# One chunk of a 31-tap convolution: from TensorE (products with diagonals) to ScalarE (products) and GpSimd (sums)

## The reference, cut to what matters

```python
zc = z[..., o4:]
glu = zc[..., :D_C] * jax.nn.sigmoid(zc[..., D_C:])
conv_c, new_c = causal_dwconv(glu, prev_c, w_conv_c)      # 31 taps, one weight per tap and channel
y_c = jax.nn.silu(layernorm(conv_c + b_conv_c, g_ln_c, b_ln_c))
```

## Time and profile before

| | |
|---|---|
| median of 3 runs | 1135.69 us (1135.05 to 1145.3) |
| profiled execution, own time | 1139.49 us |
| its span on the core | 1137.9 us |
| mean granted TensorE clock | 0.983 |
| TensorE busy | 1079.7 us, 95% of the span |
| VectorE busy | 934.3 us, 82% |
| ScalarE busy | 720.0 us, 63% |
| GpSimd busy | 97.1 us, 9% |

### The profile page before, as it was taken

How to read it: one execution, slowest core, us unless ns; L and a number is a source line. 1 busy time by engine, 2 the same in 40 slices (tenths; PEclk the granted TensorE clock), 3 DMA queues, 4 the chain that set the end, 5 groups by cost and what they waited for, 6 DMA issues and landing times.

```text
span 1137.9 us, 17514 instructions
## 1 busy us (share of the span) xinstructions
PE 1079.7 (95%) x6405; PEld 954.4 (84%) x6405; DVE 934.3 (82%) x1277; ACT 720.0 (63%) x891; POOL 97.1 (9%) x120
## 2 busy tenths in 40 slices
PE   6996999999998998799999999999999999999985
PEld 5995999999998897688888888888888888888775
DVE  6998866656668699756989989899898999999765
ACT  5434544434444532646888888888888788888562
POOL 5420000000000350100001010000100001003000
PEclk9998999999999999799999999999999999999998
DMA  8522445554452333145999999999999999999910
GB/s 331 192 90 77 148 149 205 207 186 185 158 213 101 131 141 118 48 149 186 387 366 389 360 374 396 342 410 361 379 386 346 410 359 385 377 369 398 338 67 39
DMA packets 23913, 291.56 MB, mean 256 GB/s; under 512 B 3128, under 2 KB 3160, under 8 KB 6960
## 3 DMA queue, kind: packets, MB, share of 16 engines
q1 hardware_dynamic: 20464, 279.24, 64.0%
q0 software_dynamic: 3392, 11.54, 2.9%
HBM read 283.98 MB, written 6.79 MB: 256 GB/s over the span
## 4 chain that ended last, share of the span: by engine, by line
PE 74%; DVE 16%; issue 3%; DMA 3%; ACT 2%; POOL 1%; DVEq 0%; POOLq 0%; ACTq 0%; SPq 0%
PE bank L635 14%; PE bank L639 14%; PE bank L638 14%; PE bank L680 9%; PE bank L683 9%; PE bank L684 9%; DVE wlo L1318 4%; DVE cv L1392 4%; DMA sq<-y_rows,row_id 2%; PE bank L698 1%; DVE rstd L1330 1%; PE bank L579 1%; DMA y_rows<-work 1%; PE bank L752 1%; PE bank L563 1%
## 5 line engine op out<-in xcount | busy, mean ns | idle before, releaser
L1229 DVE TENSOR_TENSOR wlo<-ring,whi 128x1024 fp32r<-128x1024 f32 x384 | 460.1, 1221 | 52.5 <-ACT whi L844 45.6
L844 ACT ACTIVATE whi<-ring 128x1024 fp32r<-128x1024 f32 x384 | 404.6, 1059 | 88.4 <-PE bank L635 76.7
L635 PE MATMUL bank<-whi,gh_hi 128*128 128x512 f32 x512 | 204.5, 399 | 0.2 <-DVE wlo L1229 0.2
L639 PE MATMUL bank<-whi,gh_lo 128*128 128x512 f32 x512 | 200.2, 391 | 0.0
L638 PE MATMUL bank<-wlo,gh_hi 128*128 128x512 f32 x512 | 199.5, 390 | 0.0
L925 ACT ACTIVATE whi<-ring 128x1024 fp32r<-128x1024 f32 x137 | 143.4, 1051 | 77.9 <-PE bank L680 75.3
L680 PE MATMUL bank<-hid_hi,whi 128*128 128x264 f32 x608 | 180.9, 297 | 9.1 <-ACT pp L936 4.8
L684 PE MATMUL bank<-hid_hi,wlo 128*128 128x264 f32 x608 | 175.2, 288 | 0.0
L683 PE MATMUL bank<-hid_lo,whi 128*128 128x264 f32 x608 | 175.1, 288 | 0.0
L1318 DVE TENSOR_TENSOR wlo<-ring,whi 128x1024 fp32r<-128x1024 f32 x137 | 166.1, 1223 | 0.4
L680 PE MATMUL bank<-gh_hi,whi 128*128 128x264 f32 x480 | 138.2, 288 | 2.8 <-DVE gh_lo L1605 1.4
(11 more groups left out here) (251 smaller groups left out, 1368.5 us busy)
## 6 DMA issues: line engine op xcount, KB each, us to landing
ring<-wstream SPq DMA_DIRECT2D x131, 2048.0 KB, 8.6
y_rows<-work POOLq DMA_DIRECT2D x7, 512.0 KB, 8.1
h<-x_in SPq DMA_DIRECT2D x1, 1056.0 KB, 5.0
y_out<-work POOLq DMA_DIRECT2D x2, 528.0 KB, 3.0
xn_rows<-work SPq DMA_DIRECT2D x2, 512.5 KB
par<-par_in SPq DMA_DIRECT2D x2, 494.5 KB, 7.0
c_sample<-xc POOLq DMA_DIRECT2D x2, 372.0 KB, 3.8
stc<-state_in SPq DMA_DIRECT2D x2, 360.0 KB, 9.2
```

Of the source, the lines that this page charges most:

```text
L635: mm = pe.matmul(out[:, :], xh, whi[:, pos, cols_], start=(k == 0), stop=False)
L639: mm = pe.matmul(out[:, :], xl, whi[:, pos, cols_], start=False, stop=(k == last))
L844: nc.scalar.activation(whi[:, q % SPLITS, :], quarter_at(q), ACT.Copy).then_inc(S["hi"], 1)
L1229: v.tensor_tensor(wlo[:, q % SPLITS, :], quarter_at(q), whi[:, q % SPLITS, :].bitcast(F32), ALU.subtract).then_inc(S["lo"], 1)
```

## The change

Chunk 0 of the convolution no longer goes through TensorE. ScalarE makes, for each tap, the product of the shifted view of `cpad` and the tap's weight: the first, with the bias, goes into `cv` itself, the other 30 into six buffers of 128x256 in `sq` (chunks 2 to 7). GpSimd adds each of the 30 to `cv`. The products come three at a time (`TAPS_ACT`) behind each of the four gelus, after the high half that precedes the square, after the layer norm's gain and behind each later high half, until 31 are made. ScalarE waits before it writes a buffer again until GpSimd has added it, and GpSimd waits for its own previous sum, since all go into the same tile. TensorE waits for the last sum ahead of the mean, in place of ScalarE's `conv_0`. The diagonals, their matmuls, and ScalarE's copy out of bank 6 go away.

```diff
-DIAGS = 12
-TAPS_PE = -(-TAPS_C // (N_ZAB - 1))
+TAPS_ACT = -(-TAPS_C // (N_ZAB - 1))
...
-        diag = sq_row[:, 2 * T:2 * T + DIAGS * P].rearrange("p (i q) -> p i q", q=P)
+        products = [sq[:, i, 0:SEQ] for i in range(2, KD)]
...
                 pool.wait_ge(S["ms"], 1)
-                for k in range(TAPS_C):
-                    if l or k >= DIAGS:
-                        pool.wait_ge(diag_used, l * TAPS_C + max(k - DIAGS + 1, 0))
-                    pool.tensor_scalar(diag[:, k % DIAGS, :], ident[:, :], col(l, "w_conv_c", k), None,
-                                       ALU.mult).then_inc(diag_ready, 1)
+                for k in range(1, TAPS_C):
+                    pool.wait_ge(tap_product, l * TAPS_C + k + 1)
+                    if k > 1:
+                        pool.wait_ge(tap_added, l * (TAPS_C - 1) + k - 1)
+                    pool.tensor_tensor(cv[:, 0, 0:SEQ], cv[:, 0, 0:SEQ], products[(k - 1) % len(products)],
+                                       ALU.add).then_inc(tap_added, 1)
...
-                tap = iter(range(TAPS_C))
-
-                def some_taps():
-
-                    for _ in range(TAPS_PE):
-                        k = next(tap, None)
-                        if k is None:
-                            return
-                        if k == 0:
-
-                            pe.wait_ge(S["glu"], 1)
-                        pe.wait_ge(diag_ready, l * TAPS_C + k + 1)
-                        pe.matmul(bank[6][:, 0:SEQ], diag[:, k % DIAGS, :], cpad[:, 0, k:k + SEQ], start=(k == 0),
-                                  stop=(k == TAPS_C - 1)).then_inc(diag_used, 1)
-
-                project(B["zab"], 2 * CB, *mix, between=some_taps)
+                project(B["zab"], 2 * CB, *mix)
...
-                pe.wait_ge(conv_0, l + 1)
+                pe.wait_ge(tap_added, (l + 1) * (TAPS_C - 1))
                 average(bank[4], D_C, average_c, S["mean"])
...
+                next_tap = iter(range(TAPS_C))
+
+                def tap_products():
+
+                    for _ in range(TAPS_ACT):
+                        k = next(next_tap, None)
+                        if k is None:
+                            return
+                        src, w = cpad[:, 0, k:k + SEQ], col(l, "w_conv_c", k)
+                        if k == 0:
+                            nc.scalar.activation(cv[:, 0, 0:SEQ], src, ACT.Identity, bias=col(l, "b_conv_c"),
+                                                 scale=w).then_inc(tap_product, 1)
+                        else:
+                            if k > len(products):
+                                act.wait_ge(tap_added, l * (TAPS_C - 1) + k - len(products))
+                            nc.scalar.activation(products[(k - 1) % len(products)], src, ACT.Copy, scale=w).then_inc(
+                                tap_product, 1)
+
+                for c in range(2 * CB):
                     high_upto(dense_quarters(B["zab"] + c))
                     act.wait_ge(acc_evac, B["zab"] + c + 1)
                     nc.scalar.activation(zb[:, c, :], ycat[:, c, :], ACT.Gelu_apprx_tanh).then_inc(S["gelu"], 1)
+                    tap_products()
                 high_upto(dense_quarters(B["zab"] + 2 * CB + 1))
+                tap_products()
                 act.wait_ge(S["centred"], 1)
...
+                tap_products()
                 for c in range(2 * CB + 2, N_ZAB):
                     high_upto(dense_quarters(B["zab"] + c))
-
-                act.wait_ge(diag_used, (l + 1) * TAPS_C)
-                nc.scalar.activation(cv[:, 0, 0:SEQ], bank[6][:, 0:SEQ], ACT.Identity,
-                                     bias=col(l, "b_conv_c")).then_inc(conv_0, 1)
+                    tap_products()
```

More of the change, by code:

```diff
@@ L204, in build @@
         spread = rstd2[:, :]
-        diag = sq_row[:, 2 * T:2 * T + DIAGS * P].rearrange("p (i q) -> p i q", q=P)
-        assert 2 * T + DIAGS * P <= KD * T
+        products = [sq[:, i, 0:SEQ] for i in range(2, KD)]
         sg = sig[:, :, :].rearrange("p b t -> p (b t)")[:, 0:512]
@@ L274, in build @@
         late_step = sem("overflow_step")
-        diag_ready = sem("diag_ready")
-        diag_used = sem("diag_used")
-        conv_0 = sem("first_chunk_convolved")
+        tap_product = sem("tap_product_ready")
+        tap_added = sem("tap_added")
         L = [{n: sem(f"{n}_{l}") for n in (
@@ L710, in _ @@
                 project(B["zc"], N_ZC, *mix, S["gh_mix"])
-                tap = iter(range(TAPS_C))
-                def some_taps():
-                    for _ in range(TAPS_PE):
-                        k = next(tap, None)
-                        if k is None:
-                            return
-                        if k == 0:
-                            pe.wait_ge(S["glu"], 1)
-                        pe.wait_ge(diag_ready, l * TAPS_C + k + 1)
-                        pe.matmul(bank[6][:, 0:SEQ], diag[:, k % DIAGS, :], cpad[:, 0, k:k + SEQ], start=(k == 0),
-                                  stop=(k == TAPS_C - 1)).then_inc(diag_used, 1)
-                project(B["zab"], 2 * CB, *mix, between=some_taps)
+                project(B["zab"], 2 * CB, *mix)
                 average(bank[5], D_B, [zb[:, c, :] for c in range(CB)], S["mean"], (S["gelu"], 1))
-                project(B["zab"] + 2 * CB, 2, *mix, between=some_taps)
+                project(B["zab"] + 2 * CB, 2, *mix)
                 pe.wait_ge(S["squared"], 1)
                 average(bank[5], D_B, [sq[:, c, :] for c in range(CB)], S["variance"])
-                project(B["zab"] + 2 * CB + 2, 3 * CA - 2, *mix, between=some_taps)
+                project(B["zab"] + 2 * CB + 2, 3 * CA - 2, *mix)
                 pe.wait_ge(S["ln_b"], CB)
@@ L963, in _ @@
                         act.wait_ge(S["glu"], 2)
-                for c in range(CB):
+                next_tap = iter(range(TAPS_C))
[14 more added lines that the diff above has]
+                for c in range(2 * CB):
                     high_upto(dense_quarters(B["zab"] + c))
```

## The result

The changed kernel takes 1165.31 us in the median (1164.14 to 1169.01, 4 runs) against 1136.61 (1135.05 to 1145.3, 4 runs): a ratio of 1.0235, 95% interval 1.0198 to 1.0273. It is slower by 2.0 to 2.7%. One execution of the kernel before took 4448.55 us in a later set of runs; the ratios leave it out.

The account below looks back on a forecast made before the run. VectorE was taken as the bound. Per layer, + 9.9 (sums) + 0.4 (late high half) - 0.4 (products with the identity) - 0.1 (TensorE's relief) = + 9.8 us; both layers + 19.6, giving 1155.3 us, range 1134 to 1174.

Parts of the forecast that it names:

- rival 2: Convolution stage: each sum holds VectorE for its whole duration, 16 to 26 us a layer, 1167 to 1187; chance 0.12.
- VectorE is the bound, TensorE's relief is worth nothing: Convolution stage: VectorE the bound by 0.3 us a chunk; TensorE's 24.8 us of taps costed at nothing.
- The sums hold VectorE, all on the chain: Convolution stage: 30 GpSimd sums a layer delay VectorE by 0.33 us each on average, 9.9 us a layer.
- the affine_select's row: GpSimd instruction over 512 elements beside a delayed VectorE tensor_scalar, from which a 0.44 us hold per sum was taken.
- The gap under a tap: Part of a hold that fits between VectorE's instructions, taken off: 0.11 us under a tap, 0.02 under a low half.
- The signs that it named: VectorE's stage groups, same counts but longer: taps 0.47 to 0.6 or 0.8 us, low halves 1.22 to some 1.5.
- The products with the identity cost 0.4 us a layer: Convolution stage: GpSimd's removed products had delayed VectorE's low halves by 0.09 us each; some 0.4 us a layer returns.
- The late high half costs 0.4 us: Seventh chunk: ScalarE's high half, behind three products, comes 1.0 us later with 0.6 to spare, adding 0.4 us.
- Sum: Whole kernel: terms give + 9.8 us a layer, + 19.6 for both, a median of 1155.3 us.
- Rival 1: Convolution stage: sums cost VectorE nothing because GpSimd gives way; 1133 to 1135 us; chance 0.24, extended to 0.19 a sum.
- Rival 3: Convolution stage: GpSimd's chain of sums becomes the bound above 1.8 us each; 1168 at 2.2; chance 0.10 with rival 4.
- Rival 4: Convolution stage: gaps halve TensorE's clock, up to 9 us more a layer, 1173; chance 0.10 together with rival 3.

Follow-up runs that it names:

- the run with other slots: Against the kernel before: ScalarE makes chunk 0's products, TensorE sums them, no GpSimd work in the stage, no taps behind the seventh chunk; 1137.27 us, ratio 0.9983.
- the half sums: Against the changed kernel: each GpSimd sum covers 128 of the 256 columns, the other half of chunk 0 left unsummed; 1146.98 us.
- the one-input run: Against the changed kernel: each GpSimd sum replaced by an in-place tensor_scalar over the same 128x256 buffer, sums left out; 1146.67 us.

## Why the prediction was right, point by point

The mechanism, the place and the direction were right. The size was not: the forecast proper was 1147 to 1163 us at 0.2 to 0.45 us a sum, and the kernel took 1165.31 at 0.45 to 0.50. The measured time lies inside the stated range of 1134 to 1174 because that range also took in part of rival 2.

- *VectorE is the bound, TensorE's relief is worth nothing.* Right, to within the few tenths of a us a layer that the run without its taps leaves open. Taking its 62 taps away changed the time by a ratio of 1.0003, and in that run, as before and after the change, no row of TensorE stands in the chain of the stage.
- *The sums hold VectorE, all on the chain.* Right in mechanism, place and sign. The step that was off is the size: 0.33 us a sum, 9.9 us a layer. It is 0.50 us in a round, and over the layer 13.4 us or 0.45 a sum. The 0.17 us that are missing in the round come from three places. The reading was taken at 0.86 ns an element from the affine_select's row (0.44 us for 512), and the held low halves show 0.55: 0.11 us. That row shows a VectorE instruction with one tensor in SBUF, the first after a wait for a DMA; no run tests whether its delay was the same hold. The gap under a tap was taken as 0.11 us and is 0.07, under a low half 0.02 and is nothing: 0.03 on average. A share of the sums was put under the evacuation, where they would be free, and none of the round's three fell there: 0.03. The signs that it named came too large as well: a low half of some 1.5 us was to be seen, and it is 1.76 in order of time.
- *The Trainium skill's figure.* The Trainium skill's "GPSIMD Engine Reference" (Performance versus the Vector engine) gives about 2.6 cycles an element for a sum, an estimate of 0.55 us here, and 13 us a layer. The runs agree with that (0.55 on a low half, 13.4 a layer), and the nearest row of the trace was the worse guide. The Trainium skill's "SBUF — State Buffer" (Who interferes with whom) is borne out where it says that only reads of GpSimd exclude a VectorE instruction with two SBUF inputs: memsets cost 0.00 us, and evacuations from PSUM kept their 0.42 us. That the other waits for the whole instruction is not: a sum, 0.74 us long in the median, held a low half for 0.55, and a one-input instruction of 0.85 us or more cost 0.17.
- *The products with the identity cost 0.4 us a layer.* They cost 0.7 (0.56 + 0.16; the run with other slots gives 0.65), and under taps they cost something in one run.
- *The late high half costs 0.4 us.* 0.67 us without sums. In the changed kernel it costs nothing, because VectorE comes later still: its low half follows its taps with no wait. ScalarE's products were hidden otherwise.
- *Sum.* + 9.8 us a layer forecast, + 12.8 measured, of which the runs account for 13.4 - 0.7 = 12.7. For the median 1155.3 us were forecast and 1165.3 measured. The sums were put 3.5 us a layer too low. By luck the products (given 0.3 too little) and the high half (0.4 too much) took 0.7 of that back.
- *Rival 1* (the sums cost nothing) and *rival 2* (the whole instruction, 16 to 26 us a layer) are out, the second by the half sums and the one-input run. In time the result is nearer to rival 2's lower edge (1167) than to the 1155 of the forecast, so the time alone could not have told them apart. Rival 1's limit of 0.19 us a sum is 11 / 60 = 0.18. *Rival 3*: a sum takes 1.0 us from start to start, at the lower end of what was expected, far from 1.8; GpSimd is not in the chain. *Rival 4*: the clock did fall, to 0.82 at the lowest, and cost nothing, since TensorE's work still fitted into the longer rounds.

## What to carry to other kernels

Work put on an idle GpSimd isn't free when VectorE is the bound and reads two operands from SBUF: count the elements that GpSimd's sums read, both inputs, at about 1.1 ns each, as VectorE's time (a one-input instruction cost about 0.65 ns an element here). Writes alone didn't count, and neither did sums beside VectorE instructions that read one operand from PSUM. Before an engine is relieved, look at whether it is in the chain; here 24.8 us of TensorE's time were worth nothing, and moving five taps the other way, from VectorE to TensorE, gained 0.35% (0.1 to 0.6).

## What the runs showed of the hardware that was not expected

- A VectorE instruction over 8 columns beside a sum took 0.69 us in place of 0.16, and 0.43 beside a half sum: the wait goes with what GpSimd reads, not with VectorE's own length.
- The hold goes both ways. Of the 15 sums in a row most take 0.74 us and the longest 1.53; the sum from 45.08 took 1.53, lay beside a low half to its end, and then the next tap took 0.95 us in place of 0.47.
- GpSimd's memset of 128x256 beside VectorE (three in 1.18 us) changed the stage by less than 0.02 us.
- With its waits on TensorE gone, GpSimd's products with the identity slowed four taps from 1.58 to 1.81 us; in the kernel before the same taps took 1.61.
- A wait of 3.0 us of TensorE for ScalarE was paid a second time at the clock of 1.2 GHz that followed it: three taps took 2.93 us where three took 1.46 just before.
